# Expert routing on one core: one-hots in another order, batches spread over other list operations, and a DRAM table with its axes turned

## The reference

```python
s = jnp.einsum('nhpc,hpkc->nhpk', q, keys)            # 8 heads x 2 sets x 128 keys
sv, si = lax.top_k(s, PEER_TOPK)                      # the 16 best of each set
comb = sv[:, :, 0, :, None] + sv[:, :, 1, None, :]
cv, ci = lax.top_k(comb.reshape(N, PEER_HEADS, PEER_TOPK * PEER_TOPK), PEER_TOPK)
i1 = jnp.take_along_axis(si[:, :, 0], ci // PEER_TOPK, axis=-1)
i2 = jnp.take_along_axis(si[:, :, 1], ci % PEER_TOPK, axis=-1)
expert = i1 * PEER_NKEYS + i2
gate = jax.nn.softmax(cv, axis=-1)
...
a = jax.nn.gelu(jnp.einsum('nd,nhkd->nhk', hb, ub), approximate=False)
return jnp.einsum('nhk,nhkd->nd', gb * a, vb)         # ub, vb: rows of the two tables of 16384 experts
```

## Time and profile before

| | us |
|---|---|
| median of 3 runs | 3335.02 (3331.49 to 3335.95) |
| the profiled execution, its own time | 3330.82 |
| its span, from the first to the last instruction | 3329.2 |
| routing, from its first transfer to the last of its copies | about 501 to 1185 |
| five periods with a placement (from L1100 to L1100 on DVE) | 83.2, 83.2, 83.6, 86.1, 85.8 |
| experts | about 1185 to 3329 |

### The profile page before, as it was taken

The page is one execution under the profiler, slowest core; times in us unless marked ns, Lnnn a source line. Parts: engine busy times, 40 slices in busy tenths (PEclk is TensorE's granted clock), DMA queues, the critical chain, the costliest instruction groups (busy, mean ns, idle before and its releaser), DMA issues.

```text
span 3329.2 us, 43974 instructions
## 1 busy us (share of the span) xinstructions
PE 3042.8 (91%) x16658; PEld 2327.8 (70%) x16658; DVE 2399.5 (72%) x4987; ACT 934.0 (28%) x1271; POOL 1490.7 (45%) x1188
## 2 busy tenths in 40 slices
PE   8899978577788569999999999999999999999997
PEld 1466644245555469998888888888888788788886
DVE  1233323998888978887778777878777777778798
ACT  0111111138878722222222222212222222212222
POOL 0010000415545333345656555666656565666453
PEclk9899988889999879999999999999999999999999
DMA  9711131602222367789999999999999999999883
GB/s 358 212 64 63 57 145 58 215 7 108 108 108 108 152 212 266 265 287 352 359 360 362 368 341 372 358 369 356 356 362 363 359 362 346 351 345 337 308 304 136
DMA packets 305919, 858.73 MB, mean 258 GB/s; under 512 B 25376, under 2 KB 108832, under 8 KB 303984
## 3 DMA queue, kind: packets, MB, share of 16 engines
q0 software_dynamic: 151344, 551.09, 45.3%
q1 hardware_dynamic: 154333, 305.79, 25.7%
q10 hardware_dynamic: 108, 0.22, 0.0%
HBM read 793.86 MB, written 63.15 MB: 257 GB/s over the span
## 4 chain that ended last, share of the span: by engine, by line
PE 54%; DMA 3%; DVE 3%; POOL 2%; issue 1%; ACT 0%; DVEq 0%; SPq 0%; ACTq 0%
PE y_ps L1889 24%; PE a_ps L1870 22%; PE picked_ps L1907 5%; PE uT_ps L1857 3%; DMA shared<-in_peer_u,ids 2%; DMA shared<-in_peer_v,ids 1%; POOL shared L1453 1%; POOL quad L1464 1%; DVE shared L1674 1%; DVE uT_lo L1615 0%; DVE shared L1644 0%; DVE shared L1657 0%; DVE v_lo L1635 0%; DVE m_lo L1630 0%; ACT uT_hi L1534 0%
## 5 line engine op out<-in xcount | busy, mean ns | idle before, releaser
L1453 POOL DMA_INDIRECT shared<-in_peer_u,ids x480 | 559.0, 1165 | 597.4 <-DVE acts L1657 507.6
L1657 DVE CUSTOM_DVE_ANT_0 shared<-shared 128x1024 f32<-128x1024 f32 x480 | 578.7, 1220 | 155.2 <-DMA shared<-in_peer_u,ids 154.8
L1870 PE MATMUL a_ps<-h_hi,uT_lo 128*128 128x320 f32 x2048 | 643.6, 314 | 1.7 <-DVE h_lo L1786 1.7
L1870 PE MATMUL a_ps<-h_hi,uT_hi 128*128 128x320 f32 x2048 | 633.7, 309 | 0.0
L1870 PE MATMUL a_ps<-h_lo,uT_hi 128*128 128x320 f32 x2048 | 633.6, 309 | 0.0
L1644 DVE TENSOR_TENSOR shared<-shared,y_ps 128x512 f32<-128x512 f32 x630 | 422.8, 683 | 162.0 <-PE y_ps L1889 161.2
L1889 PE MATMUL y_ps<-v_hi,m_lo 128*128 128x512 f32 x1280 | 510.9, 399 | 23.4 <-DVE shared L1644 11.3
L1889 PE MATMUL y_ps<-v_lo,m_hi 128*128 128x512 f32 x1280 | 504.1, 394 | 0.0
L1889 PE MATMUL y_ps<-v_hi,m_hi 128*128 128x512 f32 x1280 | 501.7, 392 | 0.0
L1464 POOL DMA_INDIRECT quad<-in_peer_v,idsT x384 | 443.4, 1155 | 117.0 <-issue 117.0
L1870 PEld LDWEIGHTS a_ps<-h_hi,uT_lo 128*128 128x128 f32 x2048 | 385.8, 188 | 7.2 <-issue 2.1
(11 more groups left out here) (187 smaller groups left out, 4187.1 us busy)
## 6 DMA issues: line engine op xcount, KB each, us to landing
shared<-in_peer_u SPq DMA_DIRECT2D x128, 512.0 KB, 7.5
v_all<-in_peer_v SPq DMA_DIRECT2D x128, 512.0 KB, 7.3
gate_blocks<-dense SPq DMA_DIRECT2D x10, 4096.0 KB, 12.1
gates<-gate_blocks SPq DMA_DIRECT2D x64, 640.0 KB, 21.9
w_ada<-in_w_ada SPq DMA_DIRECT2D x12, 2048.0 KB, 11.2
x_in<-in_x_prompt SPq DMA_DIRECT2D x16, 512.0 KB, 4.7
shared<-in_peer_u,ids POOLq DMA_INDIRECT x480, 8.5
shared<-in_w_in SPq DMA_DIRECT2D x8, 768.0 KB, 12.7
```

The source lines that it names most:

```text
L1453: pool.indirect_dma_start(out=rows[n % 4], out_offset=None, in_=u_table if n < DOTS else v_table, in_offset=bass.IndirectOffsetOnAxis(ap=i ...
L1657: nc.vector.tensor_tensor_reduce(out=rows[n % 4], in0=rows[n % 4], in1=token_row, scale=1.0, scalar=0.0, op0=ALU.mult, op1=ALU.add, accum_ ...
L1870: last = nc.tensor.matmul(a_ps[n][:, 0:GROUP], lhs[s][:, k, :], rhs[:, k, tok], start=k == 0 and m == 0, stop=k == KD - 1 and m == 2)
```

## The change

It has three parts.

1. **One-hots.** In each batch DVE makes the left one-hot before the right one.
2. **Batches.** The calls `rows(b)` stand elsewhere in DVE's list: batches 0 and 1 among the first 16 `max`, 2 to 5 among the pairs of `max_index` and `match_replace`, 6 and 7 among the second `max`, 8 and 9 among the second `max_index`, 10 to 14 in `best_pairs`, and 15 behind `slots`. Six places among the short operations of `chosen_ranks` fall away. ACT's first `widen_keys` of a period with a placement moves from batch 6 to batch 11, its Exp from batch 12 to batch 14.
3. **DRAM layout.** `gate_blocks` has the pair of keys as its outermost axis. A store then writes 64 pieces of 512 B for each partition where it wrote one of 32 KB; a load of a pair's gates reads one piece of 5 KB for each partition where it read ten of 512 B.

```diff
-                    sp.dma_start(gate_blocks[d * 2 + half, :, :, :].rearrange("p i j -> p (i j)"),
-                                 dense[half][:, :, :].rearrange("p i j -> p (i j)")).then_inc(stored[half], 16)
+                    sp.dma_start(gate_blocks[:, :, d * 2 + half, :].rearrange("c p n -> p c n"),
+                                 dense[half][:, :, :].rearrange("p (c i) j -> p c (i j)", i=2))\
+                        .then_inc(stored[half], 16)
...
-                    if choose is not None and b == 6:
+                    if choose is not None and b == (6 if placed is None else 11):
                         widen_keys(choose, 0)
-                    if choose is not None and b == 12:
+                    if choose is not None and b == (12 if placed is None else 14):
...
                     own.mark(nc.vector.max(best[:, n, low], s_ps[:, n, :]))
+                    if n % 8 == 7:
+                        rows(n // 8)
...
                     own.mark(nc.vector.match_replace(work3[:, n, :], best[:, n, low], s_ps[:, n, :], NEG))
-                rows(0)
+                    if n % 4 == 3:
+                        rows(2 + n // 4)
...
                     .then_inc(S.first_keyed, 1)
-                rows(15)
                 dve.wait_ge(S.key_wide, t * 2 + 2)
...
                                         hit[:, :, 1, :], ALU.add).then_inc(S.keyed, 1)
+                rows(15)
...
+                wait(dve, S.left, d * BATCHES + max(b - 1, 0))
+                nc.vector.tensor_tensor(left_hot[b % 2][:, :, :], key(0), keys_iota, ALU.is_equal)\
+                    .then_inc(S.left_hot, 1)
                 wait(dve, S.right, d * BATCHES + max(b - 1, 0))
...
-                wait(dve, S.left, d * BATCHES + max(b - 1, 0))
-                nc.vector.tensor_tensor(left_hot[b % 2][:, :, :], key(0), keys_iota, ALU.is_equal)\
-                    .then_inc(S.left_hot, 1)
...
-                sp.dma_start(gates[parity][:, :, :, :],
-                             gate_blocks[:, :, bass.ds(c * 2, 2), :].rearrange("n p i j -> p n (i j)"))\
+                sp.dma_start(gates[parity][:, :, :, :].rearrange("p n i j -> p (n i j)"),
+                             gate_blocks[c, :, :, :].rearrange("p n j -> p (n j)"))\
...
-        gate_blocks = nc.dram_tensor("gate_blocks", (BLOCKS, P, NKEYS, BLOCK), F32, kind="Internal").ap()
+        gate_blocks = nc.dram_tensor("gate_blocks", (NKEYS // 2, P, BLOCKS, 2 * BLOCK), F32, kind="Internal").ap()
```

More of the change, by code:

```diff
@@ L984, in two_lists @@
                     own.mark(nc.vector.max(best[:, n, high], work3[:, n, :]))
-                rows(1)
+                    if n % 8 == 7:
+                        rows(6 + n // 8)
                 own.settle()
@@ L989, in two_lists @@
                     own.mark(nc.vector.max_index(best_at[:, n, high], best[:, n, high], work3[:, n, :]))
-                rows(2)
+                    if n % 8 == 7:
+                        rows(8 + n // 8)
                 own.settle()
@@ L993, in two_lists @@
                 nc.vector.tensor_copy(best_key[:, :, :], best_at[:, :, :]).then_inc(S.best_key, 1)
-                rows(3)
             def best_pairs(t, rows):
@@ L1007, in best_pairs @@
                         ALU.add))
-                rows(4)
                 own.settle()
@@ L1013, in best_pairs @@
                         own.mark(nc.vector.max(pair[:, h, part], sums[:, h]))
-                    rows(5 + n * 3)
+                    rows(10 + n * 3)
                     own.settle()
@@ L1018, in best_pairs @@
                         own.mark(nc.vector.max_index(pair_at[:, h, part], pair[:, h, part], sums[:, h]))
-                    rows(6 + n * 3)
+                    rows(11 + n * 3)
                     own.settle()
@@ L1024, in best_pairs @@
                             own.mark(nc.vector.match_replace(sums[:, h], pair[:, h, low], sums[:, h], NEG))
-                        rows(7)
+                        rows(12)
                         own.settle()
@@ L1038, in chosen_ranks @@
                 own.mark(nc.vector.tensor_scalar(narrow[:, :, :], pair_at[:, :, :], NW, None, ALU.is_ge))
-                rows(10)
                 own.settle()
                 own.mark(nc.vector.tensor_tensor(ranks[:, :], digits[:, 2:4], digits[:, 0:2], ALU.subtract))
-                rows(11)
                 own.settle()
@@ L1046, in chosen_ranks @@
                     .to_broadcast([P, 2, HEADS, TOPK]), ALU.mult))
-                rows(12)
                 own.settle()
                 own.mark(nc.vector.tensor_tensor(ranks[:, :], ranks[:, :], digits[:, 0:2], ALU.add))
-                rows(13)
                 own.settle()
@@ L1055, in chosen_ranks @@
                 own.mark(nc.vector.tensor_copy(rank[:, 1], ranks[:, 1]))
-                rows(14)
                 own.settle()
```

## The result

| | before | after |
|---|---|---|
| median, us | 3335.48 (3331.49 to 3340.35, 4 runs) | 3373.94 (3370.5 to 3375.38, 4 runs) |
| ratio, 95% interval | | 1.0108 [1.0095, 1.0121] |
| span of the profiled execution, us | 3329.2 | 3373.8 |
| five periods with a placement, us | 83.2, 83.2, 83.6, 86.1, 85.8 | 80.5, 92.9, 92.5, 91.0, 95.7 |

The changed kernel is slower by 38.5 us, 1.1%. The forecast was slower by 16, to 3351, with a range that ended at 3364: the direction is right, the size is not.

The account below looks back on a forecast made before the run. Placement periods were taken as bound by a loop of waits, ACT's stretch plus a turn, and experts by PE. Routing +19.4 and experts -3 made +16.4 us: 3347 on the profiled execution, 3351 as median, range 3340 to 3364.

Parts of the forecast that it names:

- second period: Period with the dot products: DVE waits early for gathered rows and, uncovered, for the second `key_wide`; +4.7 us.
- first placement: ACT's first `left` no longer waits for its one-hot, and starts when `take_q` ends; -5.8 us.
- four turns: Between ACT's stretches: batch 15 behind `slots` delays the last placement and next product; 4.8 us more each.
- four stretches: From ACT's first `left` to its second `key_wide`: earlier batches remove idle time; -0.9 us each.
- after the last placement: Period without products: DVE waits early for `slotsT`, for which PE must end the last batch; +4.9 us.
- experts: Experts stage: faster gate loads win back part of PE's 10.5 idle us; -3 us, between 0 and 10.5.
- the chain to POOL's end: From ACT's second `key_wide` ending (W): `slots`, left one-hot, right one-hot, POOL's product, ending 8.1 us later.
- The clock: In each turn, PE's longer idle time slows the next first product: 1.0 us taken, between nothing and 2.9.
- The layout: DRAM layout: store takes at most 34 us, hidden at no cost; gate load lands sooner, experts gain 3 us.
- The rivals: ACT starts at its one-hot: 3316, chance 0.06; layout gives back the loss: 3339, 0.12; store becomes the loop: 3398, 0.10.
- Two signs: Profile after, if the forecast is right: loops of about 88 us and ACT's stretches of about 61.5 us.

Follow-up runs that it names:

- the run that moved batch 14: Changed kernel with batch 14 behind the short operations of `chosen_ranks`, straight ahead of its large comparison; 3371.53 us, ratio 1.0101.
- the run with 48 products: Changed kernel with PE making 48 unread products between the placements of batches 14 and 15; 3360.83 us, ratio 1.0085.
- The run with the old positions: Changed kernel with the batch calls at their positions of before, in periods without a placement only; 3361.58 us, ratio 1.0081.

## Why the prediction was right in direction and wrong in size

| term of the sum | forecast | measured |
|---|---|---|
| second period | +4.7 | +5.6 |
| first placement | -5.8 | -3.9 |
| four turns | +19.2 (4.8 each) | +23.0 (5.7 each) |
| four stretches | -3.6 (-0.9 each) | +8.4 (+2.1 each) |
| after the last placement | +4.9 | +6.4 |
| experts | -3 | +4.7 |

Measured are the differences of the two profiles; with 0.5 us ahead of the second period they make 44.7. The spans differ by 44.6, and the medians by 38.5: the profiled execution of before was 4.7 us below its median, that of after 1.4 above. The stretches are the largest miss: 12.0 us of 28.

**Batch 15: right.** The place of the cost, ACT's wait (4.95 forecast, 4.87), the chain to POOL's end (8.1 forecast, 7.95) and the first `left` straight behind `take_q` are as drawn. Both runs on it agree: 26.9 us when it alone is moved, 31.3 when it alone is put back.

**The clock: mis-sized, in another place, and partly there before.** The step took the placement at 2.02 us, from a row of batch 14 (875.04 in the earlier trace rows), and 1.0 for a slower first product. But the row for batch 15 stood in the same trace: 3.55 us behind a wait of 3.45. After the change it is 3.75, and the product does not grow (7.2 to 7.8; 7.0 to 8.1 before). PE starts the product at W + 11.6, where the step had W + 10.1; the 1.0 that was meant for the product covers part of this by luck. The step's other end was off as well: W + 6.35 before the change is one turn of four, which read 4.9, 6.35, 6.6 and 5.5, or 5.8 on average. Half a microsecond from each end makes the turns' miss of 0.9.

**The stretch: the step that failed.** The step said that each stretch gets 0.9 us shorter, because "the two buffers hold it back, not its own work". It got 2.1 us longer. The new wait of ACT for the first multiplication, 2.0 to 2.1 us in each, is that growth; the other idle time is 1.4 us a stretch, as before, so the 0.9 was not given back either.

Two things in the step were wrong. First the size: it counted 64 us of DVE work in a loop, 45.1 for the list and 19 for the one-hots, though the earlier trace rows had DVE busy for 73.7 of 83. The 32 one-hots take 31.4 us in the second placement, as most left ones last longer than 0.68 us beside POOL's product (34.2 before). Then the place: DVE's idle time in a loop lies at its start, 10.2 to 10.8 us ahead of `gateT` and 2.6 ahead of one-hot 2, which may not be made before ACT has used one-hot 0. Before, all 16 `max`, all 16 pairs, and the second lists of 16 `max` and 16 `max_index` stood ahead of one-hot 2; now only 16 `max` and four pairs do. The rest has to be done while ACT is in its stretch: DVE works for 58.8 us from one-hot 2 to the end of L1065 (for 53.7 in ACT's whole stretch before, 814.97 to 877.51). So behind one-hot 2 it is DVE's own work that sets the pace, which the step had ruled out.

The end shows it too: behind one-hot 14 come 8.5 us of work (878.95 to 887.45, with the stall of 2.1) where 5.6 stood, with a stall as well (878.50 to 884.09 in the run with batch 15 alone, which keeps the old positions). ACT needs the result after 6.5. So ACT waits 2.06 us where the result was there about 1 us ahead. That the places of batches 0 to 14, with ACT's two moves, did it is shown (that run has no such wait); that the stall at L1050 alone did it is refuted by the run that moved batch 14. How the wait divides between the order and POOL's stalls stays open, as no run takes the stalls away; a second `key_wide` buffer, which would take the wait itself away, was not tried.

The other idle time is at the start, where the first placement of a stretch takes 2.05 us, or 3.4 to 3.7 at a lower clock (0.69 over 919 to 924 in the third). It is slow in three of the four later stretches now and in two of the four before. In the run with 48 products three of the four are 63.2 to 63.3 us, in the changed kernel one, so some 1.5 us of a stretch that begins slowly hang on the clock.

**First placement: the same miss.** It starts 11.3 us after softmax (forecast 10.8) and holds 2.4 us idle instead of 0.5, of which 1.95 are the wait for the first multiplication.

**Second period and the end: right.** 2.48 + 0.73 us of waiting for rows (2.7 forecast) and 2.04 for the second `key_wide` (2.04). At the end DVE waits until W + 13.3 (W + 12.0 forecast); the placement at the lower clock, 1.7 us where 0.5 was allowed, is most of that. The run with the old positions gives back the first in full and 3.3 us of the second.

**The layout: right about the store, wrong about experts.** 16.3 us is below the bound of 34 and hidden. The gate load is twice as fast, but PE's idle time did not hang on it: from the last softmax instruction to the end it is 2146.3 us before and 2150.9 after, 2145.0 to 2153.5 over the kernels with the new layout and 2146.3 to 2151.5 over those with the old one, so neither the +4.7 nor the -3 of the forecast can be told from their spread. Here 4096 KB in 16.3 us, in pieces 640 KiB apart, are 257 GB/s where the old store made 347, a quarter less. The Trainium skill ("DMA: Bandwidth & Descriptors", section on latency and other measured facts) gives 207 GB/s for copies between HBM tensors at a pitch of 512 KiB and less at larger powers of two. The store here is above that figure, but it is not the page's own case, whose pitch lies between partitions and is a power of two, so the rule stands untested here.

**The rivals.** ACT did not begin ahead of `take_q` (824.14 and 824.64 above), the layout gave nothing back (ratio 0.9996), and no engine waited for a store: all three are refuted. Two signs that the forecast gave for being right did not come: the loops measure 91.3 to 92.5 us, not about 88, and the later stretches 63.4 to 64.9, not about 61.5.

## What to carry to other kernels

Idle time of an engine over a whole loop says nothing about the end of the loop: with two buffers it cannot be spent in advance. So count the engine's work, at its measured length, from the first instruction that is held by a buffer to the one that others wait for, and see what a new order puts between them. Where a step makes PE wait longer, price the work just behind that wait from its own row, not from a neighbour's: it may run at the lower clock already, and then the longer wait adds little. The last item of a pipelined batch is worth moving ahead of a long tail, on the engine that makes it and on the one that takes it: here that was worth 42 us against the changed kernel, and with the old positions elsewhere 0.35% against the one before.

## What the runs showed of the hardware

- A DVE operation beside POOL's product of 2.4 us can be held by it: 2.54 us instead of 0.42 (L1050), 1.18 to 2.18 instead of 0.68 (one-hots), 3.25 instead of 1.23 (L1067). Or it is POOL that is held: 4.26 us beside the large comparison of 2.28. Which operation is hit moves with the order. The Trainium skill ("SBUF — State Buffer", section on the two separate sides) says that GpSimd reading SBUF and a DVE operation with two inputs in SBUF lock one pair of ports for a whole instruction, and that the later one is blocked. These rows agree: L1067 ends 1.08 us behind POOL's product, POOL's product 2.21 behind the comparison, each close to its own length.
- The same 16 matmuls took 2.02 to 3.75 us, at granted clocks from 1.00 to 0.50, behind PE's waits of 3.4 to 3.5 us (before), and 3.75 us at 0.50 in all five placements behind waits of 10.8 to 11.0 us (after). With PE kept busy until then it was 2.02 at 1.00.
- 4096 KB in pieces of 512 B landed in 16.3 us, in pieces of 32 KB in 12.1; 640 KB in pieces of 5 KB in 11.6 us beside full queues, in pieces of 512 B in 22.3.
